# Two-layer mixture-of-experts backbone: the last four expert steps' results kept on chip and summed by TensorE

## What is computed

```python
def _moe(h, gates, w1, w3, w2):
    y = jnp.zeros_like(h)
    for e in range(N_EXPERTS):
        a = jax.nn.silu(h @ w1[e]) * (h @ w3[e])
        y = y + gates[..., e:e + 1].astype(h.dtype) * (a @ w2[e])
    return y
...
        hx = _modulate(x, sh2, sc2)
        yx = _moe(hx, _route(hx, w_router, router_bias), moe_w1[l], moe_w3[l], moe_w2[l])
        x = _layernorm(DEEPNORM_ALPHA * x + g2 * yx, ln_g[l, 1], ln_b[l, 1])
```

## Time and profile before

| | |
|---|---|
| median of three runs | 1212.03 us (1209.22 to 1213.81) |
| the profiled execution's own time | 1212.09 us |
| its span, first to last instruction | 1210.4 us |
| PE busy | 989.6 us (82%) |
| DVE, ACT, POOL busy | 326.3, 226.4, 257.2 us |
| moved over HBM | 331.42 MB, mean 274 GB/s |
| expert steps, layer 0 and layer 1 | 41 and 25 |

### The profile page before, as it was taken

The page is one execution under the profiler, slowest core; times in us unless marked ns, Lnnn a source line. Parts: engine busy times, 40 slices in busy tenths (PEclk is TensorE's granted clock), DMA queues, the critical chain, the costliest instruction groups (busy, mean ns, idle before and its releaser), DMA issues.

```text
span 1210.4 us, 24004 instructions
## 1 busy us (share of the span) xinstructions
PE 989.6 (82%) x9029; PEld 555.9 (46%) x9030; DVE 326.3 (27%) x766; ACT 226.4 (19%) x556; POOL 257.2 (21%) x483
## 2 busy tenths in 40 slices
PE   3999999999999889988886449998988768747860
PEld 1444645564665545544543224635555334423430
DVE  1003033633345222212211166105324312111115
ACT  1311112740231111101100133104412001000100
POOL 0200000010035434433331320000101314321431
PEclk9999999989899999999997869999998879978995
DMA  9994475390365784589999956527665999999942
GB/s 338 368 410 198 157 261 209 139 368 14 139 237 160 285 313 168 183 343 361 394 393 398 372 169 221 180 99 278 271 250 220 400 398 395 395 407 410 390 156 104
DMA packets 89109, 331.42 MB, mean 274 GB/s; under 512 B 10780, under 2 KB 13036, under 8 KB 64484
## 3 DMA queue, kind: packets, MB, share of 16 engines
q1 hardware_dynamic: 66500, 282.13, 60.7%
q0 software_dynamic: 21088, 47.48, 11.1%
q10 hardware_dynamic: 1472, 1.12, 0.3%
HBM read 303.18 MB, written 27.53 MB: 273 GB/s over the span
## 4 chain that ended last, share of the span: by engine, by line
PE 71%; DMA 13%; issue 8%; DVE 4%; ACT 1%; SPq 1%; POOL 1%; POOLq 0%; DVEq 0%; ACTq 0%
PE PS L1781 18%; PE PS L1542 16%; PE PS L1797 8%; PE PS L1704 7%; DMA W<-in_moe_w 5%; DMA XT<-in_moe_w 5%; PE PS L1475 3%; PE PS L1771 3%; PE PS L1508 3%; PE PS L1558 3%; PE PS L1789 2%; DMA W<-in_w_ada 2%; PE PS L1666 1%; PE PS L1654 1%; PE PS L1751 1%
## 5 line engine op out<-in xcount | busy, mean ns | idle before, releaser
L1781 PE MATMUL PS<-W,EX 128*32 128x256 f32 x2944 | 180.5, 398 | 48.0 <-issue 26.3
L1542 PE MATMUL PS<-W,XT 128*128 128x512 f32 (+1 forms) x480 | 189.1, 554 | 2.4 <-ACT XT L777 2.4
L1781 PEld LDWEIGHTS PS<-W,EX 128*32 128x32 f32 x2944 | 97.6, 114 | 116.7 <-issue 64.3
L1542 PEld LDWEIGHTS PS<-W,XT 128*128 128x128 f32 x480 | 91.1, 191 | 95.6 <-issue 93.2
L752 ACT ACTIVATE AT<-EX 64x512 f32<-64x512 f32 x64 | 40.4, 631 | 399.0 <-PE PS L1771 387.6
L650 POOL TENSOR_TENSOR RSTD<-VAR,HALF 128x1 f32<-128x1 f32 (+1 forms) x24 | 16.3, 683 | 457.7 <-DVE VAR L1056 457.7
L1781 PE MATMUL PS<-RAB,EX 128*32 128x256 f32 x640 | 83.2, 419 | 33.3 <-DMA XT<-in_moe_w 19.9
L1346 DVE COPY EX<-PS 128x256 f32<-128x256 f32 x66 | 28.0, 424 | 292.8 <-PE PS L1781 292.8
L681 POOL DMA_DIRECT2D y_rows<-AT x136 | 67.5, 497 | 174.7 <-DVE AT L1356 165.0
L1797 PE MATMUL PS<-W,AT 128*32 128x256 f32 x1472 | 95.1, 402 | 1.5 <-DVE AT L1353 1.5
L681 POOL DMA_DIRECT2D y_rows<-EX x128 | 63.5, 496 | 153.0 <-DVE EX L1356 138.9
(11 more groups left out here) (202 smaller groups left out, 1059.4 us busy)
## 6 DMA issues: line engine op xcount, KB each, us to landing
W<-in_moe_w SPq DMA_DIRECT2D x66, 2048.0 KB, 19.6
W<-in_w_ada SPq DMA_DIRECT2D x24, 2048.0 KB, 11.0
RAB<-in_moe_w SPq DMA_DIRECT2D x10, 2048.0 KB, 21.1
XT<-in_moe_w SPq DMA_DIRECT2D x10, 2048.0 KB
H<-in_moe_w SPq DMA_DIRECT2D x10, 2048.0 KB, 17.7
W<-in_w_in SPq DMA_DIRECT2D x7, 2048.0 KB, 21.2
EX<-xg_rows POOLq DMA_DIRECT2D x136, 64.0 KB, 5.7
W<-in_w_out SPq DMA_DIRECT2D x4, 2048.0 KB, 18.8
```

Source lines behind the costliest of these rows:

```text
L1542: mm = pe.matmul(ps[:, 0:cw], XT[:, k, P * t:P * t + P], w[:, k, :], start=(k == 0), stop=(k == KD - 1))
L1781: mm = pe.matmul(UP_PS[o:o + ROWS, 0:256], rows, moe_up(p, n)[:, k, 256 * a:256 * a + 256], start=(k == 0), stop=(k == KD - 1), tile_posit ...
```

## The change

The results of the last four steps of a layer stay in SBUF: `YO` has four places, and the last two blocks are no longer stored at all (the two before them are stored and not read). POOL gathers the other rows of `y_rows` while the last steps run, for tokens whose row lies in the last four blocks with row number 0 and weight 0 (`DESTE`, `WE`). The sum is made on PE, in PSUM: the gathered rows times diagonal matrices of the weights (`DIAG`, made by ACT), and the four on-chip blocks times matrices that hold a token's weight where its row stands (`OH`, made by DVE in `shares`, transposed by PE after expert 0 and copied by ACT after the last step to `OHT`). For the on-chip blocks the array is cut into four tiles of 32 rows, each writing another PSUM bank. DVE then multiplies and adds from PSUM. In layer 1 the modulation gate is multiplied into each block's result as it is evicted (`GQ`), and the residual enters the PSUM sum through the identity; `finish` takes the statistics from PSUM. The residuals beside the first three steps of layer 0 move from (0), (1), (2, 3) to none, (0, 1), (2, 3). `mix` of the four tiles stands ahead of `lam(1)` on DVE. The load of the LayerNorm parameters (`load_ln(0, 1)`) moves behind the sums in layer 0, and SP's wait ahead of the load of `f` stands for the early gathers.

```diff
...
-        YO = [AT[:, 0, 128:384], EX[:, 3, 128:384]]
+        YO = R4[:, :, :].rearrange("p a (b d) -> p (a b) d", b=2)
+        OH = [AT[:, 0, 128:256], AT[:, 0, 256:384], EX[:, 3, 128:256], EX[:, 3, 256:384]]
+        OHT = [KT[:, :].rearrange("p (t b n) -> p t b n", t=4, b=4), X[:, 2, :].rearrange("p (t b n) -> p t b n", t=2, b=4)]
+        DIAG = [w[:, :].rearrange("p (t k n) -> p t k n", t=2, k=2)
+                for w in (AB[:, :, :, :].rearrange("p a b c -> p (a b c)"), SWT[:, :, :].rearrange("p a b -> p (a b)"))]
+        ROWIDX = OVER[:, :, :].rearrange("p a b -> p (a b)")[:, 0:P].rearrange("p (b s) -> p b s", b=4)
+        WE = GM[:, 0:2, :]
+        GQ = RC[:, 1024:1280]
...
-        G2 = H[:, :].rearrange("p (b k d) -> p b k d", b=2, k=2)
+        G2 = [w[:, 2048 * n:2048 * n + 2048].rearrange("p (k d) -> p k d", k=2) for w in (RAB, H) for n in range(2)]
...
-                    for b in range(2):
-                        sp.wait_ge(g_in[b], 16 * sum(tiles(l) for l in range(key[1])))
+                    for t in range(4):
+                        g_wait(sp, key[1] - 1, t)
...
-                        with pool.If(total > n):
+                        with pool.If(total > n + 2):
                             wait_apart(pool, rows_staged[L], n + 3)
                             load_rows(n + 4, (3 + c) % 2)
                             wait_apart(pool, out_copied[L], n + 2)
-                            store_rows(n, (3 + c) % 2)
+                            store_rows(n, (3 + c) % 4)
...
+                pool.wait_ge(S["early_ready"], val("early_ready", L, 0))
+                wait_apart(pool, out_copied[L], pool.value_load(META[0:1, L, 0, NEXP:NEXP + 1], min_val=1, max_val=BLOCKS - 1))
+                through = steps_before(pool, L, NEXP - 1)
+                wait_apart(pool, up_done[L], through)
+                for t in range(T):
+                    if t == 2:
+                        wait_apart(pool, down_done[L], through)
+                    for k in range(2):
+                        pool.indirect_dma_start(out=G2[t][:, k, :], out_offset=None, in_=y_rows[0:BLOCKS * ROWS, :],
+                                                in_offset=bass.IndirectOffsetOnAxis(ap=DESTE[:, t, k:k + 1], axis=0))\
+                            .then_inc(g_in[t], 16)
                 pool.wait_ge(halves_ready, L + 1)
...
-                    if t >= 2:
-                        rstd(req(L, "ln2", t - 2), 1)
-                        pool.wait_ge(S["mixed_ready"], val("mixed_ready", L, t - 2))
-                    for k in range(2):
-                        pool.indirect_dma_start(out=G2[:, t % 2, k, :], out_offset=None, in_=y_rows[0:BLOCKS * ROWS, :],
-                                                in_offset=bass.IndirectOffsetOnAxis(ap=DEST[:, t, k:k + 1], axis=0))\
-                            .then_inc(g_in[t % 2], 16)
-                for t in range(T - 2, T):
                     rstd(req(L, "ln2", t), 1)
+                if L + 1 < DEPTH:
+                    full(pool, ("cb", L, T - 1, 3))
+                    load_ln(L, 1)
...
-            def weigh(L, t):
-                g_wait(act, L, t)
-                g0 = G2[:, t % 2, 0, :]
-                nc.scalar.activation(g0, g0, ACT.Copy, scale=WK2[:, t, 0:1]).then_inc(weighed, 1)
             for L in range(DEPTH):
                 T = tiles(L)
-                if L:
-                    weigh(L - 1, 0)
-                    weigh(L - 1, 1)
...
+                act.wait_ge(S["early_ready"], val("early_ready", L, 0))
+                for t in range(T):
+                    for k in range(2):
+                        ins = nc.scalar.activation(DIAG[t // 2][:, t % 2, k, :], IDENT, ACT.Copy, scale=WE[:, k, t:t + 1])
+                ins.then_inc(S["diag_ready"], 1)
...
+                act.wait_ge(S["affine"], val("affine", L, 0))
+                for t in range(T):
+                    key = ("oht", L, t)
+                    copy(OHT[L][:, t, :, :].rearrange("p b n -> p (b n)"), full(act, key), freed(key))
                 if L + 1 < DEPTH:
                     lambdas(L + 1)
...
+                def shares():
+                    early, first = GS[:, 0:2, 0:T], PM[:, 0, :]
+                    link(dve.tensor_scalar(T1[:, 0, :], CNT[:, 3, 16:17], float(ROWS), -4.0 * ROWS, ALU.mult, ALU.add))
+                    link(dve.tensor_scalar(early, DF[:, :, 0:T], T1[:, 0, :], None, ALU.is_lt))
+                    dve.tensor_tensor(WE[:, :, 0:T], WK2[:, 0:T, :].rearrange("p t k -> p k t"), early, ALU.mult)
+                    dve.tensor_tensor(DESTE[:, 0:T, :].rearrange("p t k -> p k t"), DF[:, :, 0:T], early, ALU.mult)\
+                        .then_inc(S["early_ready"], 1)
+                    link(dve.tensor_scalar(first, T4[:, :], 4.0 * ROWS, -4.0 * ROWS, ALU.mult, ALU.add))
+                    slots = cst("slots").rearrange("p (b s) -> p b s", b=3)
+                    dve.tensor_tensor(ROWIDX[:, 0:3, :], slots, first[:, 0:3].unsqueeze(2).to_broadcast([P, 3, ROWS]), ALU.add)
+                    link(dve.tensor_scalar(ROWIDX[:, 3, :], slots[:, 0, :], first[:, 3:4], 3.0 * ROWS, ALU.add, ALU.add))
+                    rows = ROWIDX.rearrange("p b s -> p (b s)")
+                    for t in range(T):
+                        second = (WKS, OHS)[t % 2][:, :, :, :].rearrange("p k t e -> p (k t e)")
+                        for k, place in enumerate((OH[t], second)):
+                            ins = dve.tensor_scalar(place, rows, DF[:, k, t:t + 1], WK2[:, t, k:k + 1], ALU.is_equal, ALU.mult)
+                        link(ins)
+                        dve.tensor_tensor(OH[t], OH[t], second, ALU.add).then_inc(S["late_ready"], 1)
...
+                        shares()
+                    for t in {4: ((), (0, 1), (2, 3)), 2: ((), (0,), (1,))}[T][n]:
...
+                    if L + 1 < DEPTH:
+                        dve.tensor_copy(YO[:, b, :], DOWN_PS[:, 0:256]).then_inc(out_copied[L], 1)
+                    else:
+                        dve.tensor_tensor(YO[:, b, :], DOWN_PS[:, 0:256], GQ, ALU.mult).then_inc(out_copied[L], 1)
...
+                def combined(t):
+                    for q in range(4):
+                        full(dve, ("cb", L, t, q))
+                    b = BANK["cb", L, t, 0][0]
+                    return PS[:, b:b + 4, 0:256]
+                def let_go(ins, t):
+                    ins.then_inc(freed(("cb", L, t, 0)), 1)
+                    for q in range(4):
+                        if q:
+                            dve.sem_inc(freed(("cb", L, t, q)), 1)
+                        else:
+                            read(dve, ("cb", L, t, 0))
+                by_quarter = lambda v: v.rearrange("p (q d) -> p q d", q=4)
+                def mix(t):
+                    g0 = G2[t][:, 0, :]
+                    let_go(dve.tensor_tensor(by_quarter(g0), combined(t), by_quarter(GT[:, t // 2, :]), ALU.mult), t)
+                    link(dve.tensor_tensor(X[:, t, :], X[:, t, :], g0, ALU.add))
+                    stats(L, "ln2", t)
+                    normalise(L, "ln2", t, S["ln2_norm"])
+                def finish(t):
+                    ps = combined(t)
+                    for q in range(4):
+                        ins = dve.bn_stats(ST[:, q, :], ps[:, q, :])
+                    link(ins)
+                    link(dve.bn_aggr(MV[:, t, :], ST[:, :, :].rearrange("p a b -> p (a b)")))
+                    r = req(L, "ln2", t)
+                    ask(r, 1, MV[:, t, 1:2], 1.0, LN_EPS)
+                    dve.wait_ge(ln_in, 32 * (2 * L + 2))
+                    let_go(dve.scalar_tensor_tensor(out=by_quarter(X[:, t, :]), in0=ps, scalar=MV[:, t, 0:1],
+                                                    in1=by_quarter(LNR[:, 0, :]), op0=ALU.subtract, op1=ALU.mult), t)
+                    dve.wait_ge(S["rstd_ready"], r + 1)
+                    dve.scalar_tensor_tensor(out=X[:, t, :], in0=X[:, t, :], scalar=RSTD[:, r, 0:1], in1=LNR[:, 1, :],
+                                             op0=ALU.mult, op1=ALU.add).then_inc(S["ln2_norm"], 1)
+                for t in range(T):
+                    mix(t) if L + 1 < DEPTH else finish(t)
+                if L + 1 < DEPTH:
                     lam(L + 1)
-                for c_ in (10, 11):
-                    for r in mod_streams(L, c_):
-                        read(dve, ("mod", L, c_, r))
-                def mix(t):
-                    g_wait(dve, L, t)
-                    dve.wait_ge(weighed, sum(tiles(l) for l in range(L)) + t + 1)
-                    g0, g1 = G2[:, t % 2, 0, :], G2[:, t % 2, 1, :]
-                    link(dve.scalar_tensor_tensor(out=g0, in0=g1, scalar=WK2[:, t, 1:2], in1=g0,
-                                                  op0=ALU.mult, op1=ALU.add))
-                    link(dve.tensor_tensor(g0, g0, GT[:, t // 2, :], ALU.mult))
-                    dve.tensor_tensor(X[:, t, :], X[:, t, :], g0, ALU.add).then_inc(S["mixed_ready"], 1)
```

(38 more changed lines are left out.)

88 lines of the change are left out of this document (49 added, 39 removed).

## The result

The changed kernel takes **1222.37 us** (median of 8 runs, 1218.88 to 1227.20), the kernel before took 1212.99 beside it (8 runs): a ratio of 1.0085, with a 95% interval of 1.0068 to 1.0103. It is **slower by 0.85%**, where the prediction had it 0.2% faster, and its time lies above the range. The profiled execution took 1222.08 us, its span is 1220.4.

What follows compares the result with a forecast made beforehand. PE work was taken to bound nearly all of the span, except where expert weights are late, mostly in layer 1. Terms -12.2 + 5.1 + 1.3 + 3.7 = -2.1 us gave 1210.0 us, range 1201 to 1220.

Steps and rivals of the forecast that it cites:

- The tail of layer 1: From PE's last `down` in layer 1 to the end: early gathers and sums on PE gain 12.2 us.
- Between the layers: Seam from layer 0 to layer 1: the exponential waits behind four mixes, making the seam 5.1 us longer.
- Weight loads still fill the DMA engines here, so I take 686.0: Seam after layer 0: tile 0's gathered rows land at 686.0 instead of 685.55, because of weight loads.
- The steps of layer 0: Layer 0's expert steps: 1.3 us for `copy_up` behind `shares`, and 3.7 us for PE's transposes of the weights' matrices.
- `turn_act`, at 367.85 before, waits for it: **1.3 us: After layer 0's step 0: `shares` delays `copy_up`, which ends at 369.07, and `turn_act` waits, costing 1.3 us.
- clearly more than 5 us: Sign of being wrong: layer 0's stage grows by clearly more than 5 us.
- Layer 1 absorbs its own overheads: Layer 1's expert stage: about 3.5 us of added work falls into waits for weights.
- (a): Rival: overheads hide in the steps, seam and tail, giving 1205.8, or 1202.3 with all step cost gone; chance 0.27.
- (b): Rival: layer 0's gathers become the bound beside weight loads, tile 3 landing late, time 1218.5; chance 0.10.
- an estimated half or more is left for the gathers: Layer 0's gathers beside weight loads: round-robin queues leave them half the rate or more, where nothing changes.
- (c): Rival: the 32-row tiles on PE don't overlap, in layer 0's sums and the tail, time 1242; chance 0.05.
- (d): Rival: the exponential does not hold the seam, `XT` goes after tile 0, some 17 us better, 1193; chance 0.02.

Runs made afterwards that it cites:

- all_moves_again: Changed kernel with `lam(1)` before the mixes, mask transposes behind the last `down`, tiles 1 to 3's masks late, tiles 0 and 1 transposed before the last combination; 1202.15 us.
- turn_first_again: Changed kernel with `lam(1)` before the mixes, mask transposes behind the last `down`, and tiles 0 and 1 transposed for layer 1 before the last combination; 1202.01 us.
- both_moves: Changed kernel with `lam(1)` ahead of the four mixes and the mask transposes behind each layer's last `down`; 1204.92 us.
- lam_first: Changed kernel with one edit: DVE computes `lam(1)` ahead of layer 0's four mixes instead of behind them; 1212.25 us.
- turn_last: Changed kernel with one edit: PE transposes the masks behind each layer's last `down` instead of behind the first expert step; 1212.43 us.
- old_layer0_again: Second run of layer 0 by the scheme of the kernel before, layer 1 by the changed one; 1196.62 us, ratio 0.9890 to the kernel before.
- changed_again: The changed kernel run again without any edit, in a later set; 1221.08 us, ratio 1.0097 to the kernel before.
- weights_late: Changed kernel with layer 1's weight loads issued only once layer 0's gathers have landed; 1216.25 us, one execution.

## Why the prediction was wrong

- **The tail of layer 1 (-12.2): right**, in size and in each step, the overlap of the row tiles included.
- **Between the layers (+5.1, measured +10.8 to the first XT): the mechanism was right, the size was not.** The exponential held the seam, and the four mixes stood ahead of it without gaps. The step that failed is "Weight loads still fill the DMA engines here, so I take 686.0": 0.45 us for a load that cost the gather 2.7. From that mistake came the second, which had no term at all: TensorE idle for 4.4 us, and then 2.9 us slower at the lower clock. Tile 0's sum ended 5.3 us later than forecast relative to the last `down`, with mixes 5.94 apart instead of 5.8 behind it.
- **The steps of layer 0 (+5.0, measured +7.8).** The step that failed is "`turn_act`, at 367.85 before, waits for it: **1.3 us**". VectorE's work was sized nearly right (4.8 against 4.3 us), but the copy came 2.4 late, the next `up` started as much later, and it ran at the lower clock, another 2.55: 4.9 in place of 1.3. The transposes cost 4.2 us (from 400.05, where the `up` before them ends, to 404.23) and 0.6 in the pause behind them (1.83 against 1.18), against 3.7. These make 9.7, of which 2 came back in later waits of the stage. By whole stages the experiments price the masks at 6.6 (all_moves_again against turn_first_again) and the transposes at 2.4 (both_moves against lam_first) to 3.1 (turn_last against the changed kernel). The forecast had named "clearly more than 5 us" here as a sign of being wrong, and it came.
- **Layer 1 absorbs its own overheads: open.** Its two middle stretches come to 459.2 us before, 461.8 and 460.4 in the two executions of the changed kernel, and 459.6 in old_layer0_again, whose layer 1 is the same. So the term of zero was right to 3 us, which is no more than single executions differ by. Nor was it found why the steps of layer 1 take near 250 us in some kernels and near 246 in others.
- **The rivals.** (a) did not happen: of the overheads in layer 0's steps only 2 of 9.7 us came back. (b), gathers as the bound, had the right suspect, and its 1218.5 was nearer than the forecast, but it looked at the wrong place: tiles 1 to 3 were never waited for, tile 0 was what counted. The rule of round-robin queues (the Trainium skill, "DMA: Bandwidth & Descriptors", section "Queues, rings and completion order") was used to make it small: "an estimated half or more is left for the gathers". A gather that takes 8.33 us in place of 5.59 does not speak against that; what failed was to price a slower first gather at 0.45 us all the same. (c) fell. (d) did not happen; lam_first, which makes it happen, is worth 8.9 us and not 17, since TensorE's transposes for layer 1 stand behind all four combinations.

The spans differ by 10.0 us where the sum had -2.1. Of these 12.1 us, layer 0's two terms have 8.4, layer 1's middle stretches 2.6, and 1.0 is a later start of the first step, which no edit explains.

What the sum never asked is what an idle TensorE costs beyond its idle time. Two such places, 2.55 and 2.9 us, are 5.5 of the 8.4 us by which layer 0's two terms (18.5 measured, 10.1 forecast) were too small.

## What to carry to other kernels

An overlap scheme earns its gain where nothing follows (the end of the kernel, 12.2 us) and can lose it where the next stage starts with the same queues: try it stage by stage, since the version with the old layer 0 beats both kernels, by 1.1% and 2.0%. When work is put in front of an in-order engine's small but awaited operation (here an exponential of 0.2 us), move that operation first. And when a change makes TensorE wait a few us, ask what the passes behind the wait take at the lower clock: here 1.7 to 2.9 us more where the clock fell.

## What the runs showed of the hardware

- TensorE's granted clock was 0.56 after 4.36 us of idleness (changed kernel; 4.41 in changed_again), but 0.68 after 4.36 us in lam_first; 0.57 after 1.66 and 2.30 us with 0.50 us of work between; 0.67 after 2.00 us (turn_last) and 1.00 after 1.86 us (both_moves). So the length of the last pause alone does not settle it.
- Sixteen products of 32 rows and 256 columns, on four 32-row tiles of the array, took 2.01 us, 3.7 times less than 16 times the 0.461 us of one product.
- The second row gather landed 5.4 to 5.6 us after its issue without weight loads beside it (changed kernel's layer 1, weights_late) and 8.3 beside them (changed kernel, lam_first).
- Kernels of the new scheme had, in two of the six sets of runs, some 6 us more in the steps of a layer, with answers to TensorE's work in the last step late by 3 us. The time of the kernel before did not change in these sets; it was not profiled in them. The cause is open.
